# Rows of experts multiplied on GpSimd and summed on ScalarE, instead of both on VectorE, for 32 of 42 early picks

## What is computed

```
s = jnp.einsum('chpd,hpnd->chpn', q, keys)           # 8 heads, 2 halves, 128 keys
sv, si = lax.top_k(s, K)                             # K = 16
cand = sv[:, :, 0, :, None] + sv[:, :, 1, None, :]
top_s, sel = lax.top_k(cand.reshape(C, PEER_HEADS, K * K), K)
eidx = ...                                           # 128 experts of 16384 for each token
g = jax.nn.softmax(top_s, axis=-1)
u = u_tab[eidx]
act = jax.nn.gelu(jnp.einsum('chkd,cd->chk', u, xb))
return jnp.einsum('chk,chkd->cd', g * act, v_tab[eidx])
```

## Time and profile before

| | |
|---|---|
| median of three runs | 2039.49 us |
| the profiled execution, its own time | 2039.35 us |
| its span, first to last instruction | 2037.4 us |
| TensorE busy over the span | 98% |
| VectorE, ScalarE, GpSimd busy | 72%, 49%, 51% |
| mean granted TensorE clock | 0.998 of full speed |

### The profile page before, as it was taken

One profiled execution on the slowest core, in us unless ns is written; L12 is line 12 of the kernel. 1 busy time (PEld: TensorE's weight loads), 2 busy tenths in 40 slices (PEclk: granted clock), 3 DMA queues, 4 the chain that ended last, 5 costly groups with the idle time before them and its releaser, 6 DMA issues.

```text
span 2037.4 us, 31716 instructions
## 1 busy us (share of the span) xinstructions
PE 2006.5 (98%) x11815; PEld 1800.5 (88%) x11815; DVE 1466.5 (72%) x2840; ACT 992.1 (49%) x1825; POOL 1046.5 (51%) x615
## 2 busy tenths in 40 slices
PE   9999999999899999999999999999999999999998
PEld 8746889999899999999999999999877787877787
DVE  6237538979898568889989899987686544067763
ACT  4337434367789843333333333334556642355643
POOL 3213456864445567775776777674335444411242
PEclk9999999999999999999999999999999999999999
DMA  5330225776678899999999999995312223310021
GB/s 207 81 101 12 74 93 159 252 250 229 209 264 283 317 362 378 396 380 375 356 367 371 390 377 402 353 402 212 124 63 93 88 88 104 101 34 32 22 83 63
DMA packets 152855, 435.31 MB, mean 214 GB/s; under 512 B 14464, under 2 KB 62720, under 8 KB 150528
## 3 DMA queue, kind: packets, MB, share of 16 engines
q1 hardware_dynamic: 111232, 282.29, 39.3%
q0 software_dynamic: 41472, 151.01, 19.7%
HBM read 391.28 MB, written 41.97 MB: 213 GB/s over the span
## 4 chain that ended last, share of the span: by engine, by line
PE 90%; DVE 6%; issue 1%; ACT 1%; DMA 1%; SPq 0%; POOL 0%; DVEq 0%; ACTq 0%
PE bank L525 19%; PE bank L527 19%; PE bank L526 19%; PE bank L931 4%; PE bank L933 4%; PE bank L932 4%; PE bank L912 3%; PE bank L1153 2%; PE bank L700 1%; PE wide L1176 1%; PE wide L1164 1%; PE bank L1176 1%; PE bank L794 1%; PE bank L796 1%; PE bank L795 1%
## 5 line engine op out<-in xcount | busy, mean ns | idle before, releaser
L2722 POOL TENSOR_TENSOR wl<-wraw,wh 128x1024 fp32r<-128x1024 f32 x272 | 673.2, 2479 | 702.7 <-ACT wh L1344 700.2
L1344 ACT CAST wh<-wraw 128x1024 fp32r<-128x1024 f32 x360 | 375.6, 1046 | 180.0 <-PE bank L527 150.2
L525 PE MATMUL bank<-WTH,wh 128*128 128x368 f32 x1024 | 337.2, 329 | 3.1 <-issue 3.1
L526 PE MATMUL bank<-WTL,wh 128*128 128x368 f32 x1024 | 336.5, 329 | 0.0
L527 PE MATMUL bank<-WTH,wl 128*128 128x368 f32 x1024 | 336.5, 329 | 0.0
L525 PE MATMUL bank<-AXH,wh 128*128 128x368 f32 (+1 forms) x832 | 300.5, 361 | 1.6 <-ACT wh L1344 1.6
L527 PE MATMUL bank<-AXH,wl 128*128 128x368 f32 (+1 forms) x832 | 296.8, 357 | 0.0
L526 PE MATMUL bank<-AXL,wh 128*128 128x368 f32 (+1 forms) x832 | 296.7, 357 | 0.0
L931 PE MATMUL bank<-AXH,wh 128*128 128x368 f32 x576 | 196.2, 341 | 9.4 <-issue 4.8
L525 PEld LDWEIGHTS bank<-WTH,wh 128*128 128x128 f32 x1024 | 192.3, 188 | 4.9 <-issue 4.9
L526 PEld LDWEIGHTS bank<-WTL,wh 128*128 128x128 f32 x1024 | 192.3, 188 | 0.0
(11 more groups left out here) (556 smaller groups left out, 4027.1 us busy)
## 6 DMA issues: line engine op xcount, KB each, us to landing
wraw<-in_wstream SPq DMA_DIRECT2D x360, 512.0 KB
g_scratch<-gs SPq DMA_DIRECT2D x12, 2048.0 KB, 8.5
gr<-g_scratch SPq DMA_DIRECT2D x15, 1536.0 KB
a_scratch<-tmp SPq DMA_DIRECT2D x72, 184.0 KB
tmp<-a_scratch SPq DMA_DIRECT2D x44, 184.0 KB
sq<-a_scratch SPq DMA_DIRECT2D x28, 184.0 KB
shifted<-hc_scratch SPq DMA_DIRECT2D x12, 270.0 KB, 4.8
fetched<-in_u_rows,diag POOLq DMA_INDIRECT x144
```

What stands on the lines that cost most here:

```text
L525: pe.matmul(o, w1, x1, start=n == 0, stop=False)
L526: pe.matmul(o, w1, x2, start=False, stop=False)
L1344: act.copy(wh[n % NSPLIT][:, :], wraw[n % NRAW][:, :]).then_inc(*w_hi.tell(n))
L2722: return pool.tensor_tensor(lo, src, hi.bitcast(F32), ALU.subtract)
```

## The change

Picks 0 to 9 stay as they are. For picks 10 to 41 GpSimd multiplies the row in place with the token, and ScalarE reads the product once more with the function Identity and takes the sum with its accumulator into the same column of `eact`, one pick later in the written order. VectorE does nothing for these picks. GpSimd, which also issues the fetches, now fetches two rows ahead and not three, and the fetch into a buffer waits for ScalarE's sum and not for VectorE. The fourth one-hot buffer, formerly two tensors `sq` side by side, becomes a view of one tensor, so VectorE makes it in one instruction, like the other three. The rest of the diff renames signals.

```diff
+FIRST_PICKS, EARLY_PICKS, LEAD, NEARLY, NFETCH = 10, 42, 4, 3, 6
...
+    both_sq = sb(ctx, "sq", [128, 2, T])
+    sq = [both_sq[:, i, :] for i in range(2)]
...
+    hot3 = both_sq[:, :, 0:512].rearrange("p a (i c) -> p a i c", i=4)
+    hots.append((hot3[:, 0, :, :], hot3[:, 1, :, :], hot3))
...
+    def on_pool(row):
+        return FIRST_PICKS <= row < EARLY_PICKS
+    def row_used(row):
+        return (row_act if on_pool(row) else picked).at(*ROWS[row])
...
# ScalarE
+        def total(row):
+            if not on_pool(row):
+                return
+            flat = fetched[buffer_of(row)[0]][:, :]
+            act.wait_ge(*pool_made.at(*ROWS[row]))
+            act.activation(flat, flat, ACT.Identity, accum_out=eact[:, row:row + 1]).then_inc(*row_act.tell(ROWS[row]))
         def pick():
+            total(early[0] - 1)
             early[0] += 1
         drive_routing(route, spill, spilled, scatter, pick)
+        total(EARLY_PICKS - 1)
...
# VectorE
-                if q % 4 == 3:
-                    for x in range(2):
-                        dve.tensor_tensor(hots[3][x], ...).then_inc(*hot.tell((q, x), q))
...
+                dve.tensor_tensor(hots[q % 4][2], iota_psum.unsqueeze(1).unsqueeze(1).to_broadcast([128, 2, 4, 128]),
+                                  places.to_broadcast([128, 2, 4, 128]), ALU.is_equal).then_inc(*hot.tell(q))
...
+            if on_pool(made[0] - 1):
+                return
...
# GpSimd
-                    pool.wait_ge(*picked.at(*ROWS[before]))
+                    pool.wait_ge(*row_used(before))
...
         def pick():
+            row = made[0]
             made[0] += 1
-            fetch(min(made[0] + 3, EARLY_PICKS))
+            if on_pool(row):
+                buf = buffer_of(row)[0]
+                flat = fetched[buf][:, :].rearrange("p (k d) -> p k d", k=KT)
+                pool.wait_ge(*ld_row[buf].at(row))
+                pool.wait_ge(*xtok_out.at("sbuf"))
+                pool.tensor_tensor(flat, flat, xtok, ALU.mult).then_inc(*pool_made.tell(ROWS[row]))
+            fetch(min(made[0] + (2 if on_pool(row) else 3), EARLY_PICKS))
```

More of the change, by code:

```diff
@@ L48 @@
 SHARED = 128 // EXTRA
-EARLY_PICKS, LEAD, NEARLY, NFETCH = 42, 4, 3, 6
+FIRST_PICKS, EARLY_PICKS, LEAD, NEARLY, NFETCH = 10, 42, 4, 3, 6
 NCAND = 80
@@ L193, in build_program @@
     tmp = [sb(ctx, f"tmp{i}", [128, T]) for i in range(3)]
-    sq = [sb(ctx, f"sq{i}", [128, T]) for i in range(2)]
+    both_sq = sb(ctx, "sq", [128, 2, T])
+    sq = [both_sq[:, i, :] for i in range(2)]
     tmps = tmp + sq
@@ L281, in build_program @@
     hots.append((hot2[:, 0, :, :], hot2[:, 1, :, :], hot2))
-    hots.append((*(x[:, 0:512].rearrange("p (i c) -> p i c", i=4) for x in sq), None))
+    hot3 = both_sq[:, :, 0:512].rearrange("p a (i c) -> p a i c", i=4)
+    hots.append((hot3[:, 0, :, :], hot3[:, 1, :, :], hot3))
     gates = ijg[:, 2, :].rearrange("p (h k) -> p h k", h=8)
@@ L420, in build_program @@
     st_e, ld_e = signal("st_e", 16), signal("ld_e", 16)
-    gates_blank = signal("gates_blank")
+    pool_made = signal("pool_made")
     ld_row = [signal(f"ld_row{i}", 16) for i in range(NFETCH)]
-    picked, row_gelu, row_sum_out, row_sum_mm = (
-        signal(x) for x in ("picked", "row_gelu", "row_sum_out", "row_sum_mm"))
+    picked, row_act, row_sum_out, row_sum_mm = (
+        signal(x) for x in ("picked", "row_act", "row_sum_out", "row_sum_mm"))
     idx_out, idx_step, idx_mm = signal("idx_out"), signal("idx_step"), signal("idx_mm")
@@ L1654, in picks_after @@
                     act.wait_ge(*picked.at("u", 127))
-                    act.activation(eweight, eact, ACT.Gelu).then_inc(*row_gelu.tell("all"))
+                    act.wait_ge(*row_act.at("u", EARLY_PICKS - 1))
+                    act.activation(eweight, eact, ACT.Gelu).then_inc(*row_act.tell("all"))
                 if PICKS[made[0]][0] == "gelu2":
                     act.wait_ge(*picked.at("u2", EXTRA - 1))
-                    act.activation(eweight2, eact2, ACT.Gelu).then_inc(*row_gelu.tell("extra"))
+                    act.activation(eweight2, eact2, ACT.Gelu).then_inc(*row_act.tell("extra"))
                 made[0] += 1
@@ L2325, in scatter @@
                 places = ijgT[:, 0:2, 4 * q:4 * q + 4].unsqueeze(3)
-                if q % 4 == 3:
-                    for x in range(2):
[L2328 to L2339, removed]
+                if q == 33:
+                    dve.wait_ge(*ld_e.at("all"))
+                    dve.scalar_tensor_tensor(eidx2, shared[:, 0:EXTRA], 128.0, shared[:, EXTRA:2 * EXTRA], ALU.mult,
+                                             ALU.add).then_inc(*routed.tell((1, "experts")))
+                    dve.tensor_reduce(token_of, ident.rearrange("p (t a) -> p t a", a=SHARED), AX.X,
+                                      ALU.add).then_inc(*routed.tell((1, "token")))
+                dve.tensor_tensor(hots[q % 4][2], iota_psum.unsqueeze(1).unsqueeze(1).to_broadcast([128, 2, 4, 128]),
+                                  places.to_broadcast([128, 2, 4, 128]), ALU.is_equal).then_inc(*hot.tell(q))
         spilled = [0]
@@ L2362, in pick @@
             if what == "gate2":
-                dve.wait_ge(*row_gelu.at("extra"))
+                dve.wait_ge(*row_act.at("extra"))
                 dve.tensor_tensor(eweight2, eweight2, shared[:, 2 * EXTRA:], ALU.mult).then_inc(*picked.tell("weights2"))
@@ L2366, in pick @@
             if what == "gate":
-                dve.wait_ge(*row_gelu.at("all"))
+                dve.wait_ge(*row_act.at("all"))
                 dve.tensor_tensor(eweight, eweight, egate, ALU.mult).then_inc(*picked.tell("weights"))
@@ L2825, in spill @@
                 pool.wait_ge(*gemm.at("qp", 7))
-                pool.memset(gs[0][:, :, 0:EXTRA], 0.0).then_inc(*gates_blank.tell("all"))
+                pool.memset(gs[0][:, :, 0:EXTRA], 0.0).then_inc(*pool_made.tell("all"))
             if spilled[0] == 14:
@@ L2964, in scatter @@
                 if blk == 0:
-                    sp.wait_ge(*gates_blank.at("all"))
+                    sp.wait_ge(*pool_made.at("all"))
                 sp.dma_start(gdram[:, :, blk, :], gs[blk % 2][:, :, :].rearrange("p (n i) t -> p n (i t)", i=8)).then_inc(*st_g[blk % 2].tell(blk))
```

## The result

The changed kernel takes 2054.02 us (median of 6 runs, 2053.15 to 2062.57), the kernel before beside it 2039.97 us (6 runs, 2039.02 to 2044.02): ratio 1.0075, 95% interval 1.0065 to 1.0085. The prediction was 2041.1 us, range 2034 to 2050. The span grew from 2037.4 to 2052.0 us.

What follows compares the result with a forecast made beforehand. TensorE, busy in every slice, was taken as the bound, held up by VectorE in the first third. Terms -9.0 + 1.5 + 7.2 + 1.0 + 1.0 = +1.7 us on 2039.35 gave 2041.1 us, range 2034 to 2050.

Steps and rivals of the forecast that it cites:

- The first third: First third of `drive_routing`: VectorE, relieved of picks, stops being late, giving TensorE back idle time and clock; -9.0 us.
- The second third: Second third of `drive_routing`: sums between gates and weight cast delay cast, low half and TensorE; +1.5 us, bounds -1.4 and +8.3.
- ScalarE in the last third: Last third of `drive_routing`: ScalarE's work with 16 sums, 89.2 us against 82.0, becomes the bound; +7.2 us.
- The chain of cast, low half and matmul: Last third: this chain is now as long as the scatter's period; +1.0 us.
- GpSimd in the last third: Last third: 16 products of 2.1 us bring GpSimd to 80.7 of about 91 us, hidden by ScalarE; 0 us.
- the zero for fetches: Fetches two rows ahead come 1.0 us late at worst, against GpSimd's 10 us to spare in the last third; 0 us.
- The end: After the last third: two sums and the last product's wait precede the next stage's first weight cast; +1.0 us (0 to 2.1).
- (a): Rival: fetched rows come late and GpSimd waits for them; up to +17 us, half of it gives 2049; chance 0.18.
- (b): Rival: in the first third ScalarE takes VectorE's place and keeps TensorE's gaps open; nothing gained, 2050; chance 0.15.
- (c): Rival: VectorE's lateness caused all idle time; -11.5 and -1.4 in the first two thirds, +7.2 in the last, 2033.7; chance 0.13.
- (d): Rival: GpSimd's products shut out VectorE's routing in the first two thirds; about +3 us on the forecast, 2044; chance 0.09.
- What would show it: Signs: first third about 95 us without gaps over 2 us; last about 90, ScalarE over 95% busy, TensorE idle some 8.

Runs made afterwards that it cites:

- e4: The changed kernel without ScalarE's 32 sums, a fetch waiting for GpSimd's product instead; 2043.17 us, ratio 1.0011 to the kernel before.
- e9: The changed kernel with only picks 10 to 17 moved and each sum behind the next weight cast; 2032.44 us, ratio 0.9965 to the kernel before.
- e10: e4 also without the fetches of rows 29 to 41, GpSimd multiplying what the buffers hold; 2036.11 us, ratio 0.9982 to the kernel before.
- e8: The changed kernel with only picks 10 to 25 moved and each sum behind the next weight cast; 2038.35 us, ratio 0.9988 to the kernel before.
- e5: The changed kernel without GpSimd's 32 products, ScalarE summing the rows as fetched; 2051.55 us, ratio 1.0057 to the kernel before.
- e6: The changed kernel with each sum behind the next spill's weight cast and ahead of its Gelu; 2048.91 us, ratio 1.0040 to the kernel before.

## Why the prediction was wrong, point by point

Two steps failed. It charged a sum's place in ScalarE's order in the second third only, and there too little; and it put GpSimd's added work at nothing. What follows goes term by term.

**The first third (forecast -9.0, was -3.7).** The mechanism was right: VectorE was the late engine, its one-hots are late no more, and the relief alone is worth -7.3 at its best (e4 and e9), -5.7 and -4.4 in e10 and e8, where the clock fell as well. The changed kernel is 3.5 us behind e9 (90.45 against 86.95): 1.4 us are idle time that the place of the sum makes, the rest is clock, which may be luck. Here the prediction failed: it argued by load alone, "The first has room even if 11.5 us shorter", and charged the sum's place in the second third only. Room on average does not help the copy for which TensorE waits. The forecast left ScalarE 2.5 us for "table loads, the Exp and the transposed copy"; more stays even without sums (e4), as gaps of 1.14 and 2.64 us.

**The second third (+1.5, was +4.0).** The prediction named the mechanism, the sum between gates and cast, and gave 8.3 as the far bound; the value taken was too small. e5 and e6 show it: without products it stays 93.6, behind the cast it is 89.9.

**ScalarE in the last third (+7.2).** Right in size: 88.4 in e5 against 89.2. Not right in how it reaches TensorE. The prediction had it wait for the gates "before each scatter", some 8 us "in small pieces before L912"; it idled 7.7 us, but in three gaps before L941, behind low halves. The chain of cast, low half and matmul, entered with 1.0 us, was the path, and what is left of the 9.5 us is mostly clock (0.98), for which this third had no term.

**GpSimd in the last third (0 taken).** The other step that failed: "47.05 + 16 x 2.1 = 80.7 of about 91 us, so hidden by ScalarE". The product takes 2.40 us (+4.8 us for 16); the low half at 2.39 in the earlier trace rows was a nearer row than the 2.10 of the earlier trace rows. And a busy sum leaves out the 0.16 us before each issue and the waits for rows. The load is 87.2 us plus 2 to 3 of waits, as much as ScalarE's. So no engine had the 10 us to spare on which the zero for fetches rested, and each engine's hiccup reaches the other through the chain product, sum, fetch, low half. The third came to +9.5 where the forecast had 7.2 + 1.0. That it was off by only 1.3 us here is in part luck: GpSimd's term of nothing did no harm because ScalarE's was already large and the two do not add.

**The end (+1.0, was +3.5).** ScalarE waits for the last product, then all that stands behind it is late. Timeline of ScalarE after the change:

```profile
716.58 1.06 ACT L1643 ACTIVATE fetched<-fetched 128x1024 f32<-128x1024 f32 x1 [2.49 <-POOL fetched L2878]
717.55 0.18 ACT L1643 ACTIVATION_READ_ACCUMULATOR fetched<-fetched 128x1 f32 x1
717.64 1.00 ACT L1653 COPY wide<-below_XH 128x1024 f32<-128x1024 f32 x1
718.58 1.04 ACT L1354 CAST wh<-wraw 128x1024 fp32r<-128x1024 f32 x1
```

The bound of 2.1 us counted two sums with GpSimd's product on time; GpSimd was late by 2.49. e9, with no moved pick there, has the end of before (32.3). Sums alone give 34.6 (e5). e4, without any sum, has 36.3, by another wait: TensorE stands 2.35 us for VectorE's `WTL`, and the clock is lower. So how the 3.5 us divide is not shown. Another 1.4 us is lost behind the end, with a gap of 1.07 us at 851.80; its cause is open. That stretch took 1304.0 us (e9) to 1308.6 (e6) in these kernels, so 1.4 us may mean nothing.

In all, of the 12.8 us between +1.7 and +14.5: first third 5.3, second 2.5, last 1.3, end 2.5, behind it 1.4, start -0.2. The place of the sum surely has 1.4 us of idle time in the first third and the 2.5 of the second; up to 2.1 us more in the first is clock. GpSimd's load is in the 1.3 and the 2.5 of the last third and the end, in a share that no run gives. And 1.8 us is relief that was overrated (-9.0 for -7.2 at best).

**The rivals.** (a), the rows come late: right in kind, small in size. A row came 9.4 us after its issue; with a spill between, that is just in time, without one 2.49 us late, once in the third, not three times 4.7. (b), ScalarE takes VectorE's place: right in part, 1.4 of 7.2 us are lost so as idle time, up to 3.5 with the clock. (c) was wrong, since the second third gave nothing; its sum also left out the forecast's two terms of 1.0 us, which its condition does not touch (2035.7, not 2033.7). (d), GpSimd shuts out VectorE: it happens, but no run shows that TensorE waited for it; in e9 the first third has both the products and the full gain.

**What would show it.** The sum (1.05 and 0.19) and the vanished waits for one-hots came as stated. The 104 us of the first window were to become "about 95"; they became 104 - 3.7 = 100.3, and a gap over 2 us stayed. "ScalarE busy over 95%" is 94% of the last window, since GpSimd held it up in turn.

## What to carry to other kernels

Work added to an in-order engine costs by where it stands before it costs by how much it is: the same sums behind the weight cast cost 3.8 us less in one third than in front of it. When a job is split over two engines, add up the load of both, with issues, gaps and landings, against the stage's length: here the stage took 88.4 us with ScalarE's new work alone and 89.7 with GpSimd's alone, where it had taken 81.65, and I took the second for hidden behind the first. Look also at what stands behind each wait in a queue: in e8 one fetch that waited for a sum held back a weight tile and cost 2.14 us. Move work only in the stage where the relieved engine is late: 8 of the 32 picks gave all of the gain (2032.44 us), the other 24 only cost.

## What the runs showed of the hardware

A GpSimd product of 1024 elements in place took 2.40 us, and so did the low half from two plain operands (2.39), where a product with spread operands took 2.10; the count of elements alone does not give the time, and the row that the forecast used was off by 0.3 us. The Trainium skill (GPSIMD Engine Reference, Elementwise — side-by-side cycle accounting) has 4497 ns for a GpSimd addition over 2048 elements; half of it, an estimate for 1024, is 2.25 us, nearer to the 2.40 measured here than that row was.

After equal gaps of 2.64 us on TensorE at the same place in the program, the next matmul took 0.41 us in e4 and e9 and 0.65 us in e8. The window's clock was 1.00, 1.00 and 0.97, and the first third 86.9, 86.95 and 89.75. In e6 and e10 it took 0.41 too, and yet the clock of the window was 0.98. What decided the level no run here tells; it makes single profiles of one third uncertain by up to 2.8 us.

VectorE was shut out by GpSimd in the changed kernel also at a wide operation, in its timeline:

```profile
493.86 3.86 DVE L2310 TENSOR_TENSOR spare<-selu,sie 128x2048 uint32<-128x2048 uint32 x1
```

GpSimd's low half ran from 493.17 for 2.39 us, to 495.56, and 495.56 + 2.28, the time of the same operation in the kernel before, is 497.84: it ended at 497.72. By the rule of the Trainium skill (SBUF — State Buffer, Who interferes with whom) that such a VectorE instruction waits until the GpSimd one is done, the trace agrees.
